# The last expert of a hybrid decoder block gets instruction streams of its own

## The reference

```python
def rms_norm(x, g):
    xf = x.astype(jnp.float32)
    y = xf * lax.rsqrt(jnp.mean(xf * xf, axis=-1, keepdims=True) + EPS)
    return (y * g.astype(jnp.float32)).astype(x.dtype)
...
def moe_ffn(h, w_router, b_router, w_gate_up, b_gate_up, w_down, b_down):
    ...
    gu = lax.ragged_dot(xs, w_gate_up, group_sizes) + b_gate_up[e_sorted]
    gate, lin = jnp.split(gu, 2, axis=-1)
    gate = jnp.minimum(gate, SWIGLU_LIMIT)
    lin = jnp.clip(lin, -SWIGLU_LIMIT, SWIGLU_LIMIT)
    act = (lin + 1.0) * (gate * jax.nn.sigmoid(SWIGLU_ALPHA * gate))
    out = lax.ragged_dot(act, w_down, group_sizes) + b_down[e_sorted]
    out_pairs = jnp.zeros_like(out).at[order].set(out).reshape(T, TOP_K, D)
    y = jnp.einsum("tkd,tk->td", out_pairs, gates.astype(out.dtype))
    return y.reshape(B, S, D)
...
        x = x + jnp.matmul(mixed, w_out[l])
        h = rms_norm(x, g_ffn[l])
        x = x + moe_ffn(h, w_router[l], b_router[l], w_gate_up[l], b_gate_up[l], w_down[l], b_down[l])
    return rms_norm(x, g_final)
```

## Time and profile before

| | us |
|---|---|
| median of 3 runs | 2420.41 |
| lowest, highest | 2419.99, 2421.04 |
| the profiled execution | 2419.2 |
| its span in the profile | 2417.6 |
| PE busy | 2358.1 (98%) |
| DVE, ACT, POOL busy | 1629.5, 1273.1, 374.5 |
| granted TensorE clock, mean | 0.991 |

### The profile page before, as it was taken

One profiled execution on the slowest core, in us unless ns is written; L12 is line 12 of the kernel. 1 busy time (PEld: TensorE's weight loads), 2 busy tenths in 40 slices (PEclk: granted clock), 3 DMA queues, 4 the chain that ended last, 5 costly groups with the idle time before them and its releaser, 6 DMA issues.

```text
span 2417.6 us, 40266 instructions
## 1 busy us (share of the span) xinstructions
PE 2358.1 (98%) x13219; PEld 1874.3 (78%) x13316; DVE 1629.5 (67%) x1669; ACT 1273.1 (53%) x1352; POOL 374.5 (15%) x412
## 2 busy tenths in 40 slices
PE   9999999999999999979999999999999999999996
PEld 7887777888888887967788777777777887777775
DVE  5212556767767254277788786878776987778877
ACT  5414663322223121165677675767666776667766
POOL 0000000000000001462211212112112121212110
PEclk9999999999999999989999999999999999999998
DMA  5133234354444234458999898989889997989998
GB/s 129 35 45 56 68 95 97 86 70 72 77 79 174 105 128 144 149 177 313 324 380 379 308 329 281 380 312 378 304 288 337 386 379 265 343 313 378 338 343 308
DMA packets 264764, 553.25 MB, mean 229 GB/s; under 512 B 29449, under 2 KB 76297, under 8 KB 263570
## 3 DMA queue, kind: packets, MB, share of 16 engines
q1 hardware_dynamic: 241394, 497.22, 61.5%
q0 software_dynamic: 23296, 55.03, 8.1%
HBM read 501.18 MB, written 51.02 MB: 228 GB/s over the span
## 4 chain that ended last, share of the span: by engine, by line
PE 52%; DMA 1%; issue 1%; DVE 0%; POOLq 0%; ACT 0%; DVEq 0%; ACTq 0%
PE m_y L2700 5%; PE m_y L2702 5%; PE m_y L2701 5%; PE m_gate L2702 5%; PE m_gate L2700 5%; PE m_lin L2700 5%; PE m_lin L2702 5%; PE m_gate L2701 5%; PE m_lin L2701 5%; PE m_spill L2739 4%; PE m_spill L2751 2%; PE m_turn L2684 1%; PE m_lin L2708 1%; PE m_gate L2670 1%; PE m_lin L2670 1%
## 5 line engine op out<-in xcount | busy, mean ns | idle before, releaser
L2512 DVE TENSOR_TENSOR m_w_lo<-raw,m_w_hi 128x2048 fp32r<-128x2048 f32 x382 | 868.8, 2288 | 245.0 <-ACT m_w_hi L2387 242.8
L2387 ACT CAST m_w_hi<-raw 128x2048 fp32r<-128x2048 f32 x382 | 730.9, 1914 | 352.9 <-PE m_lin L2702 243.9
L121 PE MATMUL c_bank<-h_hi_r,ring_hi 128*128 128x512 f32 x656 | 259.0, 395 | 1.9 <-DVE qk_r L1427 0.9
L2700 PE MATMUL m_gate<-m_w_hi,x_hi 128*128 128x512 f32 x508 | 215.7, 425 | 0.0
L2700 PE MATMUL m_y<-m_w_hi,m_a_hi 128*128 128x512 f32 x512 | 210.2, 411 | 1.8 <-DVE m_a_lo L2560 1.8
L2702 PE MATMUL m_y<-m_w_hi,m_a_lo 128*128 128x512 f32 x512 | 199.9, 390 | 0.0
L2701 PE MATMUL m_y<-m_w_lo,m_a_hi 128*128 128x512 f32 x512 | 199.6, 390 | 0.0
L2702 PE MATMUL m_gate<-m_w_hi,x_lo 128*128 128x512 f32 x508 | 198.8, 391 | 0.0
L2700 PE MATMUL m_lin<-m_w_hi,x_hi 128*128 128x512 f32 x508 | 198.4, 391 | 0.0
L2702 PE MATMUL m_lin<-m_w_hi,x_lo 128*128 128x512 f32 x508 | 198.3, 390 | 0.0
L2701 PE MATMUL m_gate<-m_w_lo,x_hi 128*128 128x512 f32 x508 | 198.2, 390 | 0.0
(11 more groups left out here) (425 smaller groups left out, 4628.5 us busy)
## 6 DMA issues: line engine op xcount, KB each, us to landing
raw<-in_w_gate_up SPq DMA_DIRECT2D x512, 512.0 KB, 11.3
raw<-in_w_down SPq DMA_DIRECT2D x256, 512.0 KB, 13.0
ring_raw<-in_w_in SPq DMA_DIRECT2D x31, 1024.0 KB, 9.4
gates<-work POOLq DMA_DIRECT2D x32, 256.0 KB, 4.9
work<-gates SPq DMA_DIRECT2D x8, 1024.0 KB, 7.0
v<-in_x SPq DMA_DIRECT2D x8, 512.0 KB, 5.4
r_rows<-work POOLq DMA_DIRECT2D x16, 256.0 KB, 2.8
o_rows<-v SPq DMA_DIRECT2D x8, 512.0 KB, 11.2
```

Of the source, the lines that this page charges most:

```text
L121: pe.matmul(out, left_hi(k), right_hi(k), start=first and k == kts[0], stop=False, skip_group_check=True)
L2387: act.copy(w_hi[:, p % WS].rearrange("p k b n -> p (k b n)"), raw[:, raw_slot(m)].rearrange("p k b n -> p (k b n)")).then_inc(signals.whi, 1)
L2512: dve.tensor_tensor(w_lo[:, p % WS].rearrange("p k b n -> p (k b n)"), raw[:, raw_slot(m)].rearrange("p k b n -> p (k b n)"), f32(w_hi[:, ...
L2700: pe.matmul(out, left_hi[:, kt], right_hi, start=False, stop=False, skip_group_check=True)
```

## The change

The loop keeps its order. Only the last super gets functions of its own (`last_body` on ACT and DVE; on PE two conditions):

- DVE: the second `activate` stands ahead of the last remainder (panel 11) and no longer behind it.
- PE: the second `a_turn` stands between panels 8 and 9, and no longer between 9 and 10.
- ACT: the squares of `y_tile(0)` and `y_tile(1)` stand ahead of the second `a_split`, with `y_out` as scratch; one instruction takes the roots of both behind it. The other squares write their scratch into `activations` (which now holds `gate_t` and `act_t`).
- SP: `y_tile(0)` is loaded first, then `g_final` in its five transfers, then the other seven tiles.
- DVE: three tiles are normed ahead of the sum with PE's last product, and five behind it; the four copies into `same_row` stand behind all eight tiles, not ahead of them; `stat` has a tensor of its own.

```diff
-        gate_t, act_t = sb("gate_t", [P, NW]), sb("act_t", [P, 2, NW])
+        activations = sb("activations", [P, 3, NW])
+        gate_t, act_t = activations[:, 0], activations[:, 1:3]
...
-        junk = half_slot(5, 0)
+        junk = activations[:, 0:2].rearrange("p a n -> p (a n)")
         same_row = xs[:, 0:P // SPILL].rearrange("p k c -> p (k c)")
-        stat, s_stat = xs[:, P // SPILL:P // SPILL + 3], xs[:, P // SPILL + 3]
+        stat, s_stat = sb("stat", [P, 3, TT + 1]), xs[:, P // SPILL]
...
-            sp.wait_ge(signals.wlo, count(last, 0))
+            sp.wait_ge(signals.wlo, count(last, -1))
             sp.sem_inc(signals.waits_met, 1)
-            sp.wait_ge(signals.s_gu, GU * nb + 5 * hb + OPEN)
+            sp.wait_ge(signals.s_gu, GU * nb + 4 * hb + OPEN)
             sp.sem_inc(signals.waits_met, 1)
-            sp.dma_start(g[:, :], g_final.partition_broadcast(P)).then_inc(g_loaded, 16)
-            for quarter in range(NG):
-                sp.dma_start(g_quarter[SPILL * quarter:SPILL * (quarter + 1), :],
-                             g_final[D // NG * quarter:D // NG * (quarter + 1)].partition_broadcast(SPILL)) \
-                    .then_inc(g_loaded, 16)
             sp.wait_ge(signals.scattered, last + (OPEN + 1))
             sp.sem_inc(signals.waits_met, 1)
             for i in range(TT):
+                if i == 1:
+                    sp.wait_ge(signals.wlo, count(last, 0))
+                    sp.sem_inc(signals.waits_met, 1)
+                    sp.wait_ge(signals.s_gu, GU * nb + 5 * hb + OPEN)
+                    sp.sem_inc(signals.waits_met, 1)
+                    sp.dma_start(g[:, :], g_final.partition_broadcast(P)).then_inc(g_loaded, 16)
+                    for quarter in range(NG):
+                        sp.dma_start(g_quarter[SPILL * quarter:SPILL * (quarter + 1), :],
+                                     g_final[D // NG * quarter:D // NG * (quarter + 1)].partition_broadcast(SPILL)) \
+                            .then_inc(g_loaded, 16)
                 sp.dma_start(y_tile(i), y_rows[i * P:(i + 1) * P, :]).then_inc(y_loaded[i], 16)
...
-            def root(i, rows):
+            def square(i, rows, scratch):
                 if i:
                     act.wait_ge(squared, i)
-                act.activation(junk[:, :], rows, ACT.Square, accum_out=stat[:, 0, i:i + 1]).then_inc(squared, 1)
-                act.wait_ge(squared, i + 1)
-                act.activation(stat[:, 1, i:i + 1], stat[:, 0, i:i + 1], ACT.Sqrt, bias=cst["eps"][:, :],
-                               scale=1.0 / D).then_inc(rooted, 1)
+                act.activation(scratch, rows, ACT.Square, accum_out=stat[:, 0, i:i + 1]).then_inc(squared, 1)
+
+            def root(first, stop):
+                act.wait_ge(squared, stop)
+                act.activation(stat[:, 1, first:stop], stat[:, 0, first:stop], ACT.Sqrt, bias=cst["eps"][:, :],
+                               scale=1.0 / D).then_inc(rooted, stop - first)
+
+            def early_square(i):
+                act.wait_ge(y_loaded[i], 16)
+                square(i, y_tile(i), y_out[:, :])
 
             def last_rows(hb, nb):
-                act.wait_ge(signals.wlo, count(last, 1))
-                act.sem_inc(signals.waits_met, 1)
-                act.wait_ge(signals.s_gu, GU * nb + GU * hb + OPEN)
-                act.sem_inc(signals.waits_met, 1)
-                for i in range(TT):
+                root(0, EARLY_ROOTS)
+                for i in range(EARLY_ROOTS, TT):
                     act.wait_ge(y_loaded[i], 16)
-                    root(i, y_tile(i))
+                    square(i, y_tile(i), junk)
+                    root(i, i + 1)
                 act.wait_ge(summed, 2)
-                root(TT, y_out[:, :])
+                square(TT, y_out[:, :], junk)
+                root(TT, TT + 1)
                 with act.If(hb > 0):
                     act.wait_ge(s_summed, 1)
...
+            def last_body(t):
+                hb, nb, _, _ = about(act, held, t)
+                s_sigmoid(0, hb, nb)
+                for p in range(WS):
+                    if p == 2:
+                        a_split(0, t)
+                    if p == 3:
+                        sigmoid(1, t)
+                    act.wait_ge(signals.panel_done, count(t, p))
+                    split(ORDER[TAIL[p + WS]][0], p + WS, t)
+                as_copy(0, hb, nb)
+                for i in range(EARLY_ROOTS):
+                    early_square(i)
+                a_split(1, t)
+                s_sigmoid(1, hb, nb)
+                as_copy(1, hb, nb)
+                last_rows(hb, nb)
...
                 hb, nb, hb_next, _ = about(act, held, t)
                 for p in range(MP):
...
-                    if p in (2, 4) and not tail:
+                    if p in (2, 4):
...
-            body(last, tail=True)
+            last_body(last)
...
-            def body(t, tail=False):
+            def picked_down(t, nb):
+                dve.wait_ge(signals.panel_done, count(t, 4 - MP))
+                dve.wait_ge(signals.s_dn, 4 * nb + OPEN)
+                pick_expert(1, t, signals.picked_dn)
+
+            def last_body(t):
+                hb, nb, _, _ = about(dve, held, t)
+                for p in range(WS):
+                    if p == 1:
+                        picked_down(t, nb)
+                        s_activate(0, hb, nb)
+                    if p == 2:
+                        a_split(0, t)
+                    if p == 3:
+                        activate(1, t, count(t, 3))
+                    split(ORDER[TAIL[p + WS]][0], p + WS, count(t, p + WS))
+                a_split(1, t)
+                s_activate(1, hb, nb)
+                last_rows(t, hb, nb)
+
...
             def last_rows(t, hb, nb):
-                dve.wait_ge(signals.s_gu, GU * nb + GU * hb + OPEN)
-                dve.sem_inc(signals.waits_met, 1)
-                for a in range(NG):
-                    group = slice(SPILL * a, SPILL * (a + 1))
-                    dve.tensor_copy(same_row[group, :].rearrange("p (b c) -> p b c", b=NG),
-                                     cst["ident"][group, group].unsqueeze(1).to_broadcast([SPILL, NG, SPILL])) \
-                        .then_inc(matched, 1)
                 dve.wait_ge(g_loaded, 16 * (NG + 1))
-                FIRST = 5
+                FIRST = 3
                 for i in range(FIRST):
                     norm(i)
                 dve.wait_ge(signals.scattered, t + (OPEN + 1))
                 dve.wait_ge(signals.out_listed[0], 16 * t + 16)
                 dve.wait_ge(signals.panel_done, count(t, len(TAIL) - 1))
                 dve.wait_ge(old_rows, 16)
+                dve.wait_ge(squared, EARLY_ROOTS)
...
                 for i in range(FIRST, TT):
                     norm(i)
+                dve.wait_ge(signals.s_gu, GU * nb + GU * hb + OPEN)
+                dve.sem_inc(signals.waits_met, 1)
+                for a in range(NG):
+                    group = slice(SPILL * a, SPILL * (a + 1))
+                    dve.tensor_copy(same_row[group, :].rearrange("p (b c) -> p b c", b=NG),
+                                     cst["ident"][group, group].unsqueeze(1).to_broadcast([SPILL, NG, SPILL])) \
+                        .then_inc(matched, 1)
                 invert(TT)
...
-            body(last, tail=True)
+            last_body(last)
...
+                    if p == 4 and tail:
+                        pe.wait_ge(signals.alo, 2 * t + (OPEN + 1))
+                        pe.wait_ge(signals.s_copied, 2 * nb + hb + OPEN)
+                        a_turn(1, t)
...
-                    if p == 6:
+                    if p == 6 and not tail:
                         pe.wait_ge(signals.alo, 2 * t + (OPEN + 1))
                         pe.wait_ge(signals.s_copied, 2 * nb + hb + OPEN)
                         a_turn(1, t)
-                        if not tail:
-                            pe.wait_ge(signals.spill_in, t + (OPEN + 1))
-                            xs_turn(hb_next)
+                        pe.wait_ge(signals.spill_in, t + (OPEN + 1))
+                        xs_turn(hb_next)
```

52 lines of the change are left out of this document (20 added, 32 removed).

## The result

The changed kernel has a median of 2425.61 us (20 runs, 2422.16 to 2432.14). The kernel before, run beside it on the same chips, has 2421.2 (20 runs). The ratio is 1.0018 with a 95% interval of 1.0012 to 1.0024, so it is slower by about 4.4 us. The forecast was 2423.0 with a range up to 2424.8. The measured time lies 0.8 above that range; the sign was right, the size was 2.6 of 4.4. Of the distance from 2423.0 to 2425.61, 0.8 is that the kernel before took 2421.2 in these rounds and not 2420.41; the other 1.8 belongs to the change. Four single executions of the later rounds took 4,833 to 13,053 us (one each of the kernel before, e1, e7 and f3), and no ratio counts them.

The account below looks back on a forecast made before the run. PE was busy 98%, but the end hung on DVE. PE restarting 1.15 us later and a clock loss of 1.4 made the last tile 2.6 later; on the median of 2420.41 that gives 2423.0, range 2420.3 to 2424.8.

Parts of the forecast that it names:

- What bounds, and the free edits: PE is busy 98% and its work doesn't grow; in the tail, the earlier second activation and transposes cost nothing.
- that rival: Tail's end: if the copies cost over 1.3 us, the scatter waits for the ninth tile; a few tenths, no own chance.
- `g_final` behind tile 0 (SP): SP's queue in the tail: five transfers, 640 KB, delay tile 1 by 1.75 us, bounds nothing to 2.1.
- tile 1 in time: Rival, SP's queue: `g_final` doesn't delay tile 1, PE restarts 0.6 earlier, last tile 0.55 earlier, 2419.9 us; chance 0.12.
- PE's restart: PE ahead of its last 24 matmuls: restarts 1.15 us later, after a gap of 3.1 where there were 1.77.
- The clock: PE's last 24 matmuls: the gap drops the granted clock to half speed, costing 1.4 us, bounds 0 and 1.85.
- two leading cases: Tail, tile 1 late in both: clock falls, 2423.0 us, chance 0.52; clock holds, 2421.6 us, chance 0.30.
- DVE: DVE in the tail: waits for PE after three tiles, then sum and five tiles; last tile normed 2.6 us later.
- The store of the last tile takes 2.69: Behind the last norm: the last store takes 2.69 us as before, ending at 2414.25.
- The later tiles land up to 1.75 later: Loads behind tile 1: up to 1.75 us later, tile 7 near 2403.2, at no cost here.
- The two rivals that forecast no loss: Tail: clock holds, 2421.6 us, chance 0.30; tile 1 lands in time, 2419.9 us, chance 0.12.
- the forecast's 4.8 us: Whole kernel: a measurement tells about 0.2%, 4.8 us, from no change; chance of staying within 0.2% was 0.95.

Follow-up runs that it names:

- e1: The changed kernel with all five `g_final` transfers again ahead of every `y_rows` load: 2422.99 us, ratio 1.0011 to the kernel before.
- e7: The changed kernel with five tiles, not three, normed ahead of the sum with PE's product: 2423.33 us, ratio 1.0008 to the kernel before.
- f3: The kernel before with the second activation and transposes moved earlier, and stores of half the columns (half the output left out): 2418.71 us, ratio 0.9984.
- e2: The changed kernel with ACT's second rounding again ahead of both early squares: 2424.03 us, ratio 1.0009 to the kernel before.
- e4: The changed kernel with sixteen extra matmuls filling PE's gap behind panel 9: 2424.26 us, ratio 1.0014 to the kernel before.
- e8: The changed kernel without the four small quarter loads of `g_final`: 2428.22 us, ratio 1.0028 to the kernel before.
- h0: The changed kernel, unaltered, profiled once more: 2425.24 us in one execution, with the kernel before at 2425.16.
- h2: The changed kernel without the four quarter loads of `g_final`, profiled once more: 2428.57 us in one execution, with the kernel before at 2425.16.
- f1: The changed kernel without quarter loads, its big load reading 128 different rows of `h_rows` (output wrong): 2426.07 us, ratio 1.0018 to the kernel before.
- h3: The changed kernel without quarter loads, big load from 128 different rows, profiled once more: 2427.13 us in one execution, kernel before at 2425.16.
- h1: The changed kernel with the big `g_final` load in front and only its four quarter loads behind tile 0: 2424.42 us in one execution, kernel before 2425.16.
- e5: The kernel before with only SP's order changed, the five `g_final` transfers behind tile 0: 2424.09 us, ratio 1.0008.
- e3: The changed kernel with `g_final` in front of all `y_rows` loads and the second rounding between the two squares: 2422.29 us, ratio 1.0004 to the kernel before.
- e6: The kernel before with only the second activation and the transposes moved earlier: 2421.53 us, ratio 0.9997.
- f4: The kernel before with each of SP's eight stores cut to half its columns (half the output left out): 2421.06 us, ratio 0.9993.
- f2: The changed kernel with the five `g_final` transfers behind tile 1 in place of tile 0: 2423.81 us, ratio 1.0009 to the kernel before.

## Why the prediction was right in its mechanism and too small

*What bounds, and the free edits.* Right. PE's busy share stays 98% and its work is the same. The second activation ends at 2394.17 and the transposes at 2394.88, both long before the rounding; nothing waits for either. The ninth tile ended at 2419.35 and was still hidden behind the store that landed at 2420.44, so that rival did not come.

The measured time is above the stated range because two terms of the sum were too small, the delay of tile 1 and the last store. The bounds were also added up wrongly: by their own terms (delay 1.3, clock 0.5; delay 2.1, clock 1.85, sum 0.3 late) they are 2421.65 and 2424.0, not 2421.0 and 2424.2.

*"`g_final` behind tile 0 (SP). [...] I take 1.75, near the stream's rate, since four of the five are small."* This is the step that failed, by its size: 1.75 was taken and 2.80 measured. Tile 1 landed 2.80 later, beyond the upper bound of 2.1, and by the start of the second square it was 2.0 to 2.8 later in the seven profiles with one big load and the late place (after, e2, e4, e7, e8, h0, h2). I had priced 640 KB by the stream's mean. But the copy of one row takes about 0.7 us longer than 128 rows would (f1, h3), and that four of the five are small is beside the point, as beside the big one they cost nothing (e8), though alone they hold tile 1 up by their issue (h1). The bound was taken from the landings of ordinary tiles, and the big load is not one. Of the forecast's rivals "tile 1 in time" rested on the contrary, that many reads of one row may be served quicker; the rows show them slower.

*PE's restart.* The arithmetic from the landing on was right: 2398.61 + 0.03 + 1.05 gives the rounding at 2399.69, and PE restarts 1.73 behind it, as before. The root starts at 2401.57, directly behind the table load (2400.28 + 1.28). So the drain of 1.38 that the Trainium skill adds to the load ("ScalarE: Activation LUTs", What ACT_TABLE_LOAD costs) does not show here either. From a landing 2.8 late instead of 1.75, PE is 2.05 late instead of 1.15.

*The clock.* Right in this profile, 1.33 against 1.4, and e4 shows the cost by removing it. Of the two leading cases the one in which it falls came in. But that the size fits within 0.1 is luck: over the kernels here the cost was from 0 to 2.8, and the upper bound of 1.85 was too low.

*DVE.* Right: it waits 2.35 for PE with three tiles before it, five tiles of 1.40 behind the sum, the last normed 3.41 later. 2.6 was forecast, and the difference is mainly the 0.9 of the restart. e7, with five tiles, waits 1.02 although PE ends 1.23 later: the wait hangs mostly on the three.

*"The store of the last tile takes 2.69" and "The later tiles land up to 1.75 later [...] no cost".* Wrong by 0.76. It took 3.45 in this profile. I treated the store as a constant. The stream that `g_final` lengthens can make it longer: e5, with all norms unchanged, has 4.1. But that is not what the 0.76 of the kernel after is. There the transfers have a pause ahead of the last five stores:

```profile
2410.00:2411.00 1.00, 0.00 (x0) 0.00 (x0) 0.96 (x3) 1.00 (x3) 0.00 (x0) 1.00 0.15 61
2411.00:2412.00 1.00, 0.00 (x0) 0.00 (x0) 0.96 (x3) 0.48 (x3) 0.00 (x0) 0.59 0.06 25
```

The first three of the five take 2.69 each, as before; only the last two are longer, 3.12 and 3.45. And the last store takes 3.44 to 3.46 in ten profiles of kernels built on the changed one (after, e1, e3, e7, e8, f1, h0 to h3), with `g_final` in front or not, with one row or 128. What the last store meets there is a packet of another kind (packets, MB and share, from the transfers of the kernel after between 2417.0 and 2420.5, by queue):

```profile
q14 instruction: 1, 0.01, 0.6%
```

And at its end it waits for one DMA engine of the sixteen (a share of 0.06):

```profile
2419.50:2420.00 0.50, 0.00 (x0) 0.00 (x0) 0.00 (x0) 0.00 (x0) 0.00 (x0) 0.50 0.06 25
```

In all ten this load of 8 KB of instructions comes 1.1 us behind the issue of the last store. In the kernel before it comes 3.9 us ahead of that issue, and the engines finish the last store together. But the load itself takes only about 0.3 us (0.6% of 3.5 us on sixteen engines), the four copies on DVE fall into the same moment in all ten, and no run parts the two. So how the 0.76 comes about is open. That it doesn't hang on the place of `g_final` is shown, by e1.

The sum by the measured terms is 2.05 + 1.33 + 0.76 = 4.1, against the 4.4 of the medians. The two rivals that forecast no loss fail for one reason each: the clock did not hold, and tile 1 was not in time. e1 tells what the second would have given: PE early, last tile at 22.17, and no gain at the end, since `xg` and the stores were next. The 0.55 that I had given it was wrong too. And the forecast's 4.8 us, as the least that can be told from no change, was too much: 20 executions of each kernel tell 4.4.

No version here that stores its whole output is shown to beat the kernel before: e6 comes nearest, at 0.9997 (0.9988 to 1.0006). What would be next is the transfers of the last 25 us.

## What to carry to other kernels

An operation that is moved ahead of another on an in-order engine takes its wait along: price a moved square by when its tile lands and by who stands behind it, and the transfer that is moved ahead of that tile by all its bytes, and small ones by the time of their issue. Before calling an engine's earlier finish a gain, look whether the transfers have a pause in that stretch; where they have none, the last store can take the gain back (all of it in e6, half in e2). A load that is far ahead of need is not free to move to a later place, if that place is in the busiest stretch of the queue.

## What the hardware did that I had not expected

**The length of the gap alone did not decide the clock.** In e5 PE has the gap of the kernel before, 1.77, restarts at full speed, and the clock falls while it works:

```profile
2399.01 0.50 PE L2705 MATMUL m_y<-m_w_hi,m_a_hi 128*128 128x512 f32 x1 [1.77 <-DVE m_a_lo L2565]
```

```profile
2399.00:2400.00 1.00, 0.99 (x4) 0.86 (x5) 0.43 (x2) 1.00 (x1) 0.00 (x0) 1.00 1.02 414
2400.00:2401.00 1.00, 1.00 (x5) 0.77 (x4) 0.32 (x2) 0.99 (x3) 0.00 (x0) 0.76 1.04 426
...
2402.00:2403.00 1.00, 1.00 (x3) 0.74 (x3) 0.96 (x3) 0.97 (x3) 0.00 (x0) 0.50 1.08 434
```

In h3, with a longer gap, it holds at full:

```profile
2401.88 0.50 PE L2734 MATMUL m_y<-m_w_hi,m_a_hi 128*128 128x512 f32 x1 [2.57 <-DVE m_a_lo L2582]
```

```profile
2402.00:2408.00 6.00, 5.61 (x24) 4.30 (x24) 4.46 (x7) 5.81 (x15) 0.00 (x0) 1.00 1.02 412
```

And in e7, with 3.52, PE works at half speed for about six microseconds:

```profile
2398.43 0.79 PE L2738 MATMUL m_y<-m_w_hi,m_a_hi 128*128 128x512 f32 x1 [3.52 <-DVE m_a_lo L2586]
```

```profile
2399.00:2404.00 5.00, 5.00 (x13) 3.92 (x12) 4.86 (x8) 4.90 (x11) 0.00 (x0) 0.50 1.03 410
2404.00:2405.00 1.00, 1.00 (x4) 0.75 (x4) 0.96 (x3) 0.97 (x3) 0.00 (x0) 0.74 1.02 418
```

So a gap of 1.77 cost nothing in two profiles (before, f4) and 1.6 in a third (e5); one of 2.03 cost 1.6 (h1), one of 2.57 nothing (h3). In all six profiles with a gap of 2.99 to 3.76 the clock fell, and the cost was 1.3 to 2.8. With no gap, or one under 1 us, it did not fall (e2, e3, e4, e6; e1, f2). What else decides is open. The Trainium skill ("TensorE: Matmul & The Clock Gate", Part 1: The HAM clock gate) says that the gate judges activity in windows that run freely and don't start with the kernel's work. That would fit one gap with two outcomes, but no run here shows it.

**One row for 128 partitions is slow.** 512 KB from one row of 4 KB landed 2.7 to 3.0 behind the tile before it (e8, h2), from 128 rows 1.3 to 1.5 behind (f1, h3). Whether the reads of one place are the limit or something else in that form of transfer was not tried.

**A store's time is not its own.** The same last store of 512 KB took between 2.7 and 5.2 us from issue to landing. Where the transfers had no pause ahead of it, it took 3.85 to 5.2 (e2, e4, e5, e6, f2); with a pause, or at least a dip in the DMA share, it took 2.7, or 3.45 where an instruction load and the copies fell into it. In e6 it had to wait at the end for one or two of the sixteen DMA engines alone.
